# w_out, norm and router of a hybrid block: one tile after another, or skewed over three tiles

## The reference, cut to what matters

```python
mix_x = merged @ lp['w_out']                      # (2048, 1024) @ (1024, 1024)
x = x + g1x * mix_x
hx2 = rmsnorm(x, norm2_g[i]) * (1.0 + sc2x) + sh2x
aff = jax.nn.softmax((h @ router_w).astype(jnp.float32), axis=-1)    # h is hx2, router_w (1024, 16)
top_val, top_idx = lax.top_k(jnp.swapaxes(aff, 1, 2), cap)           # the next stage
```

## Time and profile before

| what | value |
|---|---|
| median of the runs | 5463.45 us |
| span of the profiled execution | 5461.6 us |
| PE busy, share of the span | 4437.8 us, 81% |
| w_out product of the first tile starts | 3506.63 us |
| last write of `affT` starts | 4053.28 us |
| start of the `w_out` product to the next tile's, mean of 15 | 34.15 us |

### The profile page before, as it was taken

One profiled execution on the slowest core, in us unless ns is written; L12 is line 12 of the kernel. 1 busy time (PEld: TensorE's weight loads), 2 busy tenths in 40 slices (PEclk: granted clock), 3 DMA queues, 4 the chain that ended last, 5 costly groups with the idle time before them and its releaser, 6 DMA issues. The chain is left out here.

```text
span 5461.6 us, 49486 instructions
## 1 busy us (share of the span) xinstructions
PE 4437.8 (81%) x17543; PEld 2775.5 (51%) x17543; DVE 1386.0 (25%) x2250; ACT 815.7 (15%) x1538; POOL 733.6 (13%) x663
## 2 busy tenths in 40 slices
PE   7598887899999998772999999766640499999994
PEld 5344443899999443331444444333320366677772
DVE  1422221455555222323000000011139411111112
ACT  0244432222222100011000000000000000000002
POOL 0022222222222000012000000011110000000000
PEclk9799999999999999895999999877765799999997
DMA  6311111211111101544100010211130044555554
GB/s 250 121 48 51 52 42 39 74 58 58 58 58 43 47 12 45 152 128 144 39 25 25 25 40 25 76 62 61 61 142 0 20 169 169 172 174 173 173 173 145
DMA packets 252137, 468.01 MB, mean 86 GB/s; under 512 B 18947, under 2 KB 124075, under 8 KB 251951
## 3 DMA queue, kind: packets, MB, share of 16 engines
q1 hardware_dynamic: 212751, 349.76, 18.9%
q0 software_dynamic: 20560, 70.83, 4.7%
q10 hardware_dynamic: 18768, 46.67, 2.4%
HBM read 356.57 MB, written 110.62 MB: 86 GB/s over the span
## 5 line engine op out<-in xcount | busy, mean ns | idle before, releaser
L1666 PE MATMUL bank<-hT,gw 128*128 128x512 f32 x1536 | 678.1, 594 | 15.0 <-DMA bw<-in_w_branch_c 11.6
L1970 PE MATMUL bank<-xeT,wgu 128*128 128x256 f32 x3072 | 667.2, 380 | 14.6 <-ACT xeT L1940 14.6
L1970 PEld LDWEIGHTS bank<-xeT,wgu 128*128 128x128 f32 x3072 | 583.0, 190 | 96.3 <-issue 18.5
L500 PE MATMUL bank<-hT,wq 128*128 128x512 f32 (+1 forms) x1216 | 513.4, 578 | 9.2 <-DMA wq<-in_w_in 6.9
L1666 PEld LDWEIGHTS bank<-hT,gw 128*128 128x128 f32 x1536 | 292.5, 191 | 385.9 <-issue 385.9
L500 PEld LDWEIGHTS bank<-hT,wq 128*128 128x128 f32 x1216 | 237.6, 198 | 254.9 <-issue 248.9
L1981 PE MATMUL bank<-wd,hid_e 128*128 128x512 f32 x768 | 333.9, 594 | 22.1 <-DVE hid_e L1914 22.1
L1168 PE MATMUL bank<-hT,wh 128*128 128x512 f32 x768 | 336.6, 598 | 12.6 <-DMA wh<-in_w_in 9.6
L1775 PE MATMUL bank<-wo,mt 128*128 128x512 f32 x512 | 264.9, 683 | 24.3 <-DMA mt<-mg_d 23.7
L1697 DVE TENSOR_TENSOR pr<-sg_m,bank 128x512 f32<-128x512 f32 x96 | 66.0, 688 | 833.0 <-ACT sg_m L1682 833.0
L1981 PEld LDWEIGHTS bank<-wd,hid_e 128*128 128x128 f32 x768 | 144.8, 190 | 204.4 <-issue 175.9
(11 more groups left out here) (279 smaller groups left out, 4887.8 us busy)
## 6 DMA issues: line engine op xcount, KB each, us to landing
wgu<-in_exp_w_gate SPq DMA_DIRECT2D x16, 3072.0 KB, 23.2
wgu<-in_exp_w_up SPq DMA_DIRECT2D x16, 3072.0 KB, 30.4
wd<-in_exp_w_down SPq DMA_DIRECT2D x16, 3072.0 KB, 13.5
ada<-in_ada_w SPq DMA_DIRECT2D x12, 2048.0 KB, 9.1
gw<-in_w_in SPq DMA_DIRECT2D x27, 512.0 KB, 5.6
fa_d<-az ACTq DMA_DIRECT2D x48, 264.0 KB
sp_in<-fa_d SPq DMA_DIRECT2D x66, 192.0 KB, 4.1
kT<-kT_d SPq DMA_DIRECT2D x36, 256.0 KB, 2.8
```

Of the source, the lines that this page charges most:

```text
L500: last = pe.matmul(PS[u % 4][:, 0:width(n)], wq[:, kind, k, :], hT[:, k, toff(n):toff(n) + width(n)], start=(k == 0), stop=(k == KD - 1))
L1666: pe.matmul(g[:, :], gw[:, b, j, k, :], hT[:, k, toff(n + 1):toff(n + 1) + TW], start=(k == 0), stop=(k == KD - 1))
L1970: last = pe.matmul(PS[4 + f % 2][:, g * CAP:(g + 1) * CAP], wgu[:, b, g, k, f * P:(f + 1) * P], xeT[:, k, :], start=(k == 0), stop=(k == K ...
```

## The change

The loop is gone: the 16 tiles are written out on every engine. PE's order for tile t is now: first half of `w_out` of t, router of t-2, second half of t, transpose of `ex` of t-2, transposes of `h2` of t-1. DVE, ACT and POOL follow the same skew. `x1`, `h2` and `s1` have three buffers, `sqx` has one. The stores of `x1` and `h2` move from ACT's queue to SP's. At the start `mt` of the first two tiles is loaded first, then `w_out` in two halves with a semaphore each, and the router's weights and the final gain only after that.

```diff
-                            if b == 1:
-                                pe.wait_ge(wo_mm, at * 2 + 2)
-                                pe.sem_inc(mt_free, 1)
-                            tail(i, j, at + 1)
+                    for t in range(TILES + 2):
+                        if t < TILES:
+                            if t % 2 == 0:
+                                pe.wait_ge(mt_in[t // 2 % 2], 16 * (t // 4 + 1))
+                            if t >= 2:
+                                pe.wait_ge(g_ok, 2 * t - 2)
+                            if t == 0:
+                                pe.wait_ge(wo_in[0], 16)
+                            out_half(t, 0)
+                        if t >= 2:
+                            route(t - 2)
+                        if t < TILES:
+                            if t == 0:
+                                pe.wait_ge(wo_in[1], 16)
+                            out_half(t, 1)
+                        if t >= 2:
+                            turn_aff(t - 2)
+                        if 1 <= t <= TILES:
+                            turn(t - 1)
```

The waits inside the three functions that stand between the halves and behind them:

```diff
+                    def turn(t):
+                        pe.wait_ge(h2_ok, t + 1)
+                        if t >= 1:
+                            pe.wait_ge(h2_cp, t)
...
+                    def route(t):
+                        pe.wait_ge(h2_cp, t + 1)
+                        if t == 0:
+                            pe.wait_ge(rw_in, 32)
+                        if t >= 1:
+                            pe.wait_ge(ex_ok, t)
...
+                    def turn_aff(t):
+                        pe.wait_ge(aff_ok, t + 1)
+                        if t >= 1:
+                            pe.wait_ge(affT_ok, t)
```

DVE, ACT and POOL in the new order, and SP's start and loop:

```diff
+                    for t in range(TILES + 2):
+                        if t < TILES:
+                            gated(t, 0)
+                        if t >= 2:
+                            softmax(t - 2)
+                        if t < TILES:
+                            gated(t, 1)
+                        if t >= 2:
+                            dve.wait_ge(aff_tr, t - 1)
+                            dve.tensor_copy(affT[:, (t - 2) * P:(t - 1) * P], PS[7][0:NE, 0:P]).then_inc(affT_ok, 1)
+                        if t < TILES:
+                            scaled(t)
...
+                    for t in range(TILES + 2):
+                        if t >= 2:
+                            exponent(t - 2)
+                        if 1 <= t <= TILES:
+                            to_sbuf(t - 1)
+                        if t < TILES:
+                            rms(t)
...
+                    load_mt(0)
+                    for c in range(2):
+                        sp.dma_start(wo[:, :, c * 512:(c + 1) * 512], w[:, :, c * 512:(c + 1) * 512]).then_inc(wo_in[c], 16)
+                    load_xt(0)
+                    load_xt(1)
+                    load_mt(1)
...
+                    for t in range(TILES):
+                        sp.wait_ge(x1_ok, t + 1)
+                        sp.dma_start(x1_d[t * P:(t + 1) * P, :], x1[:, t % XB, :]).then_inc(x1_st[t % XB], 16)
+                        if t + 2 < TILES:
+                            load_xt(t + 2)
+                        if t % 2 == 1 and t // 2 + 2 < TILES // 2:
+                            sp.wait_ge(wo_mm, 2 * t + 2)
+                            load_mt(t // 2 + 2)
+                        sp.wait_ge(h2_ok, t + 1)
+                        sp.dma_start(h2_d[t * P:(t + 1) * P, :], h2[:, t % HB, :]).then_inc(h2_st[t % HB], 16)
```

More of the change, by code:

```diff
@@ L1736, in _, with load_mt @@
                 def _(sp):
[L1737 to L1746, removed]
+                    def load_mt(m):
+                        sp.dma_start(mt[:, m % 2], mg_d[:, :, m * 2 * P:(m + 1) * 2 * P].rearrange("k p t -> p k t")).then_inc(mt_in[m % 2], 16)
@@ L1748, in _, with out_half @@
+                    for b in range(XB):
+                        sp.wait_ge(x1_st[b], 16 * len(range(b, TILES, XB)))
+                    for b in range(HB):
+                        sp.wait_ge(h2_st[b], 16 * len(range(b, TILES, HB)))
                 @block.tensor
                 def _(pe):
[L1750 to L1754, removed]
+                    def out_half(t, c):
@@ L1755, in tail @@
                         for k in range(KD):
-                            last = pe.transpose(PS[4 + k // 4][:, k % 4 * P:(k % 4 + 1) * P], h2[:, b, k * P:(k + 1) * P], eye[:, :])
-                        last.then_inc(h2_tr, 1)
-                        pe.wait_ge(h2_cp, at + 1)
+                            last = pe.matmul(PS[2 * (t % 2) + c][:, :], mt[:, t // 2 % 2, k, t % 2 * P:(t % 2 + 1) * P], wo[:, k, c * 512:(c + 1) * 512],
+                                             start=(k == 0), stop=(k == KD - 1))
@@ new lines, in out_half @@
+                        last.then_inc(wo_mm, 1)
+                    def turn(t):
+                        pe.wait_ge(h2_ok, t + 1)
+                        if t >= 1:
+                            pe.wait_ge(h2_cp, t)
+                        for k in range(KD):
+                            last = pe.transpose(PS[4 + k // 4][:, k % 4 * P:(k % 4 + 1) * P], h2[:, t % HB, k * P:(k + 1) * P], eye[:, :])
+                        last.then_inc(h2_tr, 1)
+                    def route(t):
[4 more added lines that the diff above has]
+                            pe.wait_ge(ex_ok, t)
@@ L1759, in tail @@
                         for k in range(KD):
-                            last = pe.matmul(PS[6][:, 0:NE], h2T[:, b, k, :], rw[:, k, :], start=(k == 0), stop=(k == KD - 1))
+                            last = pe.matmul(PS[6][:, 0:NE], h2T[:, t % 2, k, :], rw[:, k, :], start=(k == 0), stop=(k == KD - 1))
                         last.then_inc(lg_mm, 1)
-                        pe.wait_ge(aff_ok, at)
-                        pe.transpose(PS[7][0:NE, 0:P], ex[:, b, :], eye[:, :]).then_inc(aff_tr, 1)
@@ L1765, in _ @@
[L1765 to L1777, removed]
-                            if b == 1:
-                                pe.wait_ge(wo_mm, at * 2 + 2)
-                                pe.sem_inc(mt_free, 1)
-                            tail(i, j, at + 1)
+                    def turn_aff(t):
+                        pe.wait_ge(aff_ok, t + 1)
+                        if t >= 1:
+                            pe.wait_ge(affT_ok, t)
+                        pe.transpose(PS[7][0:NE, 0:P], ex[:, t % 2, :], eye[:, :]).then_inc(aff_tr, 1)
@@ L1783, in _ @@
                 @block.vector
                 def _(dve):
[L1785 to L1809, removed]
```

100 lines of the change are left out of this document (61 added, 39 removed).

## The result

The changed kernel takes 5179.89 us in the median of four runs (5179.65 to 5186.77), against 5457.56 before (four runs, 5445.21 to 5466.5): a ratio of 0.9498, 95% interval 0.948 to 0.9515, 277.7 us less. The forecast was 5194, and the range 5178 to 5240 holds the result.

The account below looks back on a forecast made before the run. The stage was taken to be bound by one tile's serial chain, 34.15 us a tile, and afterwards by PE's own work. Middle 266.0 plus start 3.5 saves 269.5 us: 5463.45 - 269.5 = 5194, range 5178 to 5240.

Parts of the forecast that it names:

- PE's own work bounds the tile: Steady tile on PE: product 13.73, router 1.79, transposes 0.89, transpose of `ex` 0.20, together 16.61 us.
- The choice for the router: Router's 16 records on PE, taken at 0.112 us each like the transposes: 1.79 us, bounds 0.8 and 3.6.
- Borders: Four borders between kinds of PE work a tile: taken at nothing, upper bound 18 us over 16 tiles.
- The chain has 7 us of room: `h2` ready some 9.8 us after a tile's second half; PE wants it at 16.6 + 0.2: slack 7 us.
- The clock stays up: Steady tiles, case as summed: PE runs without a stop at clock 1.00; 5194, chance 0.77.
- rival (b): Clock still falls once a tile, in transposes or router: 2.8 us more a tile, 5236; chance 0.09.
- The start: Start of stage, `mt` and half of `w_out` loaded first: PE starts at 3503.1, 3.5 us saved, bounds 1.5 and 8.4.
- the second lands 7.1 us after the first: Start loads: first half of `w_out` lands 7.1 us after `mt`, which takes 7.6 us.
- the bound at which bytes alone decide: Start loads at the rate of `w_out`, 3/4 of 13.0 us: PE starts at 3498.2, saving 8.4; 5189, chance 0.1.
- some 2 us: Start loads: estimated latency of each load that a queue hides, from 2 and 4 MB differing by 3.9 us.
- The fit of the Trainium skill: Start loads at 2 us plus bytes at 436 GB/s: landed 9.2 us after issue, forecast 5188; not used.
- Queue, buffers, code: SP's stores and third buffers cost nothing; rivals: SP's queue bounds, 5264, chance 0.05; written-out code too slow, 5514, 0.02.

Follow-up runs that it names:

- the skew over two tiles: Changed kernel with PE doing both halves of t, then transposes, router and softmax transpose of t-1 in one piece: 5241.56 us, ratio 0.9621.
- the written-out serial kernel: The kernel before with the stage's loops written out and nothing else: 5451.87 us, ratio 1.0001.

## Why the prediction was right

**PE's own work bounds the tile.** Right. 16.61 us forecast, 16.51 measured: product 13.82 for 13.73, router 1.71 for 1.79, transposes 0.87 for 0.89, the transpose of `ex` 0.11 for 0.20. The choice for the router, which had no row at the high clock, holds: its 16 records go at 0.107 us each, the transposes at 0.109, as if the weight load that both have set the rate. Its lower bound, 0.8 us for "its columns alone", follows from no row; at 0.429 us for 512 columns it would be 0.2 us.

**Borders.** Taken at nothing, and next to nothing it is: PE is busy for 234.00 of 234.00 us, and all that a border can have cost is in the product's 0.09 us.

**The chain has 7 us of room.** Right. 7.8 us in the trace; 4.8 more on POOL change nothing in the middle, 14.4 more make POOL's round the bound.

**The clock stays up.** Right for this kernel, 1.00 over the whole steady part; rival (b) is out. But it was nearer than it looked: in the skew over two tiles, a tail of 5.7 us with two waits of 1.2 and 1.3 us brings a part of it, 1.7 us a tile.

**The start.** The step that was mis-sized: "the second lands 7.1 us after the first". 3.5 us were put down, 7.3 measured, near the bound at which bytes alone decide. Two things were wrong. The part that a queue hides was put at "some 2 us", but the working beside it leaves more: if 2 MB more cost 3.9 us, 9.1 - 3.9 = 5.2 us of a 2 MB load are fixed, the second load lands 3.9 us after the first, and the start is 11.5 us, where 10.9 were measured. And the 7.6 us of `mt` were taken for the price of 1 MB, as they were in the comparison with the Trainium skill. They are not. Timeline of before, one such load, and a stretch of it (columns as in rows 4):

```profile
3560.91 0.37 ACTq L1823 DMA_DIRECT2D x_d<-x  x1
3560.92 0.33 SPq L1746 DMA_DIRECT2D xt<-in_x  x1
...
3561.92 0.38 SPq L1744 DMA_DIRECT2D mt<-mg_d  x1
```

```profile
3563.00:3569.00 6.00, 1.97 (x8) 1.57 (x8) 1.28 (x1) 0.21 (x2) 2.34 (x1) 0.50 1.03 380
```

A store of `x1` and the load of `xt`, 1 MB together, go out 1 us ahead of `mt`, and then the DMA engines are busy throughout, at 380 GB/s. So 2 MB share that time. This load landed 7.1 us after its issue, 8.1 after the first of the three, where 3 us and 2.6 us a MB give 8.2. A load of 1 MB by itself was not measured.

The fit of the Trainium skill (DMA: Bandwidth & Descriptors, "Anatomy of one DMA") gave an estimate of 9.2 us for these 3 MB, and the trace has 10.9; it was nearer than the 14.7 of the sum. That fit of the Trainium skill is for DMAs issued by GpSimd, and these loads are issued by SP. Measured here are 3 us and 2.6 us a MB, some 400 GB/s, where the fit has 2 us and 436 GB/s.

**Queue, buffers, code.** All free, as said, with one reserve: on ACT's queue the stores would cost 1.8 us at the end. The instruction fetch rule (the Trainium skill, Runtime: NRT & Kernel Launch, "Instruction fetch mechanics") agrees with what the written-out serial kernel shows: 1.0 us less for the stage, and no tile that stands out. In before, the transposes behind each of the loop's three borders come 34.4 us after those of the tile ahead, all others 33.9 to 34.2; written out, all come 33.9 to 34.2.

**The sum.** 269.5 forecast, 276.4 in the trace: 3.8 more at the start, 2.6 in the middle, 0.5 at the end. Of the middle 1.5 are the tile's 0.1 us. The other 1.1 is how long the first product stays at the low clock, 15.7 us up to DVE's second half and not 16.8; in the seven other kernels whose steady tile is the same, the middle is 261.1 to 261.8, so that part is this execution's.

The time came out 14 us below the forecast: 8.2 us are gain beyond the sum, 6.9 of them in the stage, and 5.9 are the time before, 5463.45 in the runs that the forecast started from and 5457.56 with the fourth. Neither has to do with the mechanism. The range ended 2 us lower, so that it held is in part luck.

## What to carry to other kernels

Where one engine's stream holds a serial chain between two pieces of its own dense work, count from the trace how long the chain is and put that much work of other items between its links, not only ahead of the first one: here a skew over two tiles left 62 of 278 us on the table, for two waits of 1.3 us and the clock behind them. What gets skewed is hidden in the steady part alone; whatever is added to the chain comes out at the end, whole or more. A load's time in a profile is its own price only if nothing else was on the DMA engines. And before a third buffer or another queue is credited, take it away again: in the steady part both did nothing here.

## What the runs showed of the hardware

A short sparse stretch is enough to cost TensorE clock. With PE idle 1.2 and 1.3 us inside 5.7 us of tail, the product behind was slower by 1.4 us in the tile shown (15.15 for 13.7) and by 1.2 to 3.0 in the others; the granted clock was 0.90 from 3600 to 3700 us of that trace, so some of it ran at 1.2 GHz. With the serial tail filled until no idle spell was longer than 0.5 us, it was still slower by up to 1.8 us in ten tiles of fifteen, and not in the other five. With transposes and router set between half products and no idle time, it never fell in 234 us. Which property of the tail does it was not separated.

On one queue, loads issued back to back ran at 2.6 us a MB from 2 to 5 MB, with rows of 1, 2 and 4 KB.

A step of DVE can be held up by POOL. DVE's scaling of `ex` (128x16, in SBUF) takes 0.23 us in every steady tile of the changed kernel. Where one of POOL's adds runs beside it, it lasts until that add ends: 1.54 us at the end of the changed kernel, 0.53 us with two more adds on POOL (it ends at 3643.50, the add at 3643.48), up to 2.12 us with six. DVE's product with the gate, which reads a PSUM bank, kept its 0.69 us beside the same adds.
